# Last MLP, second layer: both halves of positions take weight rows 0 and 1, then both take rows 2 and 3

## The chip, the cores and the metric

One core of a Trainium2 chip runs the whole program. The time is the device time of one execution in microseconds (us). Fewer is better. The kernel before took 1864.22 us (median of 3 runs, 1864.22 to 1864.34).

## The reference

The program computes three blocks on 512 positions of width 1024, in float32: a convolutional mixer with a gated MLP, a retention layer with an MLP, and a chunked attention layer with an MLP, with a final RMS norm. The change touches only the last MLP, and of it only the second matrix product:

```python
def _sqrelu_mlp(h, w1, w2):
    u = jax.nn.relu(h @ w1)
    return (u * u) @ w2
...
        h = h + _sqrelu_mlp(_rmsnorm(h, mlp_norm_g[i]), mlp_w1[i], mlp_w2[i])
    return _rmsnorm(h, final_norm_g)
```

Here `w1` is 1024 x 4096 and `w2` is 4096 x 1024.

## The kernel before, in words

Every float32 product is made of three matmuls: an operand is split into a high part (`_hi`, float32r) and a low part (`_lo`, what is left), and `product` (lines 688 to 690) issues hi x hi, hi x lo and lo x hi into the same PSUM bank. ScalarE (ACT) makes the high part of a weight block (line 1198), GpSimd (POOL) subtracts it from the weights to make the low part (line 667).

The last MLP goes in 4 chunks ("turns") of 1024 hidden columns. A chunk first makes its hidden columns (8 units of 24 matmuls), then its second layer (`seven_products`), which is a 2 x 2 block product done with seven products instead of eight. Their names, in order, are b11, b21, t1, b22, t2, t3 and t4. Each has a weight block of 4 rows of 128 x 512 (k = 0 to 3), held in one of the two slots of `w_hi` and `w_lo` in turn, and 256 positions in two halves of 128. A unit is one half with all four rows, 12 matmuls, with its own PSUM bank. The units of a chunk are numbered u = 0 to 13 (b11 is 0 and 1, b21 is 2 and 3, t1 is 4 and 5, and so on).

Four PSUM banks serve these units: two (one for each half) for b11, t2, t3 and t4, two for b21, t1 and b22. So two products that follow each other, such as b21 and t1, use the same two banks. After each unit TensorE (PE) signals `unit_done`, VectorE (DVE) adds the bank into the result in SBUF (line 1941, 128x512; line 1939 where it is the first) and signals `unit_taken`; the next unit on that bank waits for it (`pe.wait_ge(unit_taken, ...)`).

DVE works in the order of `seven_rows` (line 1927 on): the add of u, and between these adds
- after u = 2 `from_psum` (line 1862, two instructions), which turns the copy of a weight block in PSUM (`in_psum`, written by ACT at line 1272) into the block of t2,
- after u = 4 and 5 `psum_lo` (line 1868), the low part of t2's rows 0 and 1, and of its rows 2 and 3, each after ACT's high part; after u = 5 `from_psum` again, for t4,
- after u = 8 and 9 `psum_lo` for t4,
- in the last chunk, from u = 10 on, `end_rows`: the sums of squares, the root and the scaling by the final norm (lines 1888, 1904, 1875 to 1883), row block by row block.

ACT converts two blocks ahead, one conversion behind each unit (`after_unit`, `convert`). A weight slot may be overwritten in rows 0 and 1 once both halves have passed them, which PE signals with `half_used`, and in rows 2 and 3 when the block is done. The blocks of raw weights are loaded by SP's queue.

All engines run their own list in order, written out by the loops of the source; nothing schedules them.

Of the kernel before, what the change touches and what calls it, by code (L numbers as in the profile page):

```python
# [24 lines left out]
P = 128  # L25
# [12 lines left out]
MLP_CHUNKS = 4  # L38
# [56 lines left out]
IN_A = ("b11", "t2", "t3", "t4")  # L95
# [69 lines left out]
def build(nc, phases, x_in, w_in, w_out, w_gate, w_up, w_down, ret_w_in, ret_w_out, att_w_in,  # L165
# [4 lines left out]
    with ctx:  # L170
# [36 lines left out]
        ps = ctx.enter_context(nc.psum_tensor("ps", [P, 8, SEQ], F32))  # L207
# [5 lines left out]
        ms, root, rc, t4 = (cols[:, 4 * k:4 * k + 4] for k in range(4))  # L213
# [48 lines left out]
        def operand(kind, k):  # L262

            if kind in ("b21", "t4"):
                cut = slice(0, 256) if kind == "b21" else slice(256, 512)
                return hh[:, k, cut], hl[:, k, cut]
            if kind in ("t1", "t2"):
                cut = slice(0, 256) if kind == "t1" else slice(256, 512)
                return hh[:, 4 + k, cut], hl[:, 4 + k, cut]
            n = ("b11", "t3", "b22").index(kind)  # L270
            return combined_hi[:, n, k, :], combined_lo[:, n, k, :]
# [22 lines left out]
        def sem(name):  # L294
            sems.append(ctx.enter_context(nc.semaphore(name)))
            return sems[-1]
# [8 lines left out]
        t_lo = sem("t_lo")  # L305
# [9 lines left out]
        w_hi = sem("w_hi")  # L315
        w_lo = sem("w_lo")
        unit_done = sem("unit_done")
        unit_taken = sem("unit_taken")
# [29 lines left out]
        half_used = sem("half_used")  # L348
# [29 lines left out]
        n_blocks = len(plan)  # L378
# [12 lines left out]
        rows_turn = plan[:rows_from].count("b11")  # L391

        def by_rows(b):

            return b >= rows_from and plan[b] in QUARTERS
# [286 lines left out]
        def _(pe):  # L682
            c = Counts(pe, sems)
            banks = [4]

            def product(o, a, b, first, last):

                nc.tensor.matmul(o, a[0], b[0], start=first, stop=False, skip_group_check=True)  # L688
                nc.tensor.matmul(o, a[0], b[1], start=False, stop=False, skip_group_check=True)  # L689
                return nc.tensor.matmul(o, a[1], b[0], start=False, stop=last, skip_group_check=True)  # L690

            def low(ahead):

                behind = lows[c.unit.n + ahead] - (c.unit.n + ahead)
                return c.unit.value(ahead + behind)

            def weights(slot, width):
                return [t[:, slot, :].rearrange("p (k c) -> p k c", c=width) for t in (wh, wl)]
# [151 lines left out]
            def quarter(kind, turn, half, banks_of):  # L850

                if kind in ("t2", "t4"):
                    pe.wait_ge(t_lo, 4 * turn + (1 if kind == "t2" else 3) + half)
                else:
                    pe.wait_ge(w_lo, low(1))
                back = {"b11": 4, "b21": 4, "t2": 8}.get(kind, 2)
                pe.wait_ge(unit_taken, c.unit.value(1 - back))
                w = weights(c.unit.n // 2 % 2, 512)
                bank = banks_of["a" if kind in IN_A else "c"][half]
                opens, ends = kind in ("b11", "b21", "t1"), kind in ("b21", "b22", "t4")  # L860
                ready = {"b11": a11_ready, "b21": a12_ready, "t4": a12_ready}.get(kind, s_ready)
                for m in range(2):
                    for k in range(4):
                        if half == 0 and m == 0:
                            pe.wait_ge(ready, 4 * turn + k + 1)
                        d = P * (half + 2 * m)
                        mm = product(ps[:, bank, 256 * m:256 * (m + 1)], [t[:, k, d:d + P] for t in w], operand(kind, k),
                                     opens and m == 0 and k == 0, ends and k == 3)
                mm.then_inc(unit_done, c.made(unit_done))
                c.unit.n += 1  # L870

            def quarter_rows(kind, turn, half, banks_of):

                def weights_ready(rows):
                    if kind in ("t2", "t4"):
                        pe.wait_ge(t_lo, 4 * turn + (1 if kind == "t2" else 3) + rows)
                    else:
                        pe.wait_ge(w_lo, low(1 + rows))

                back = {"b11": 4, "b21": 4, "t2": 8}.get(kind, 2)  # L880
                pe.wait_ge(unit_taken, c.unit.value(1 - back))
                w = weights(c.unit.n // 2 % 2, 512)
                bank = banks_of["a" if kind in IN_A else "c"][half]
                opens, ends = kind in ("b11", "b21", "t1"), kind in ("b21", "b22", "t4")
                ready = {"b11": a11_ready, "b21": a12_ready, "t4": a12_ready}.get(kind, s_ready)
                for k in range(4):
                    if half == 0:
                        if k % 2 == 0:
                            weights_ready(k // 2)
                        pe.wait_ge(ready, 4 * turn + k + 1)  # L890
                    positions = [t[:, P * half:P * (half + 1)] for t in operand(kind, k)]
                    mm = product(ps[:, bank, :], positions, [t[:, k, :] for t in w], opens and k == 0, ends and k == 3)
                    if half == 1 and k == 1:
                        mm.then_inc(half_used, c.made(half_used))
                mm.then_inc(unit_done, c.made(unit_done))
                c.unit.n += 1

            def turn_x(part, turn):

# [8 lines left out]
            def seven_products(turn):  # L908

                n = c.unit.n  # L910
                banks_of = {"a": (n % 4, (n + 1) % 4), "c": ((n + 2) % 4, (n + 3) % 4)}
                for kind in QUARTERS:
                    for half in range(2):
                        if turn >= rows_turn:
                            quarter_rows(kind, turn, half, banks_of)
                        else:
                            quarter(kind, turn, half, banks_of)
                    if turn == rows_turn + TURN_X_IN and kind in ("t3", "t4"):
                        turn_x(int(kind == "t4"), turn)
# [4 lines left out]
            for f in phases:  # L924
                if f == "mix":
# [3 lines left out]
                    for u in range(4, MIX_UNITS):  # L929
                        unit8(X)  # L930
                        for g in taps_after(u):
# [3 lines left out]
                            for m in range(2):  # L935
                                mm = nc.tensor.matmul(ps[:, 6 + m, :], tap_w[:, g % 4, m, :], upad[:, 2 + m, g:g + SEQ],
                                                      start=g == 0, stop=g == TENSOR_TAPS - 1, skip_group_check=True)
# [5 lines left out]
                    for t in range(4):  # L943
                        mm = nc.tensor.matmul(ps[:, 5, :], ones[:, :], cacc[:, t, :], start=t == 0, stop=t == 3,
                                              skip_group_check=True)
# [199 lines left out]
        def _(act):  # L1145
            c = Counts(act, sems)
# [6 lines left out]
            def convert(n=1):  # L1153

                for _ in range(n):
                    place = c.of[w_hi]
                    halves = place.n
                    if place.turn is None and halves >= 2 * n_blocks:
                        return
                    if place.turn is None and halves >= 2 * rows_from and halves % 2 == 0 and not held:  # L1160
                        b = halves // 2
                        if by_rows(b) != by_rows(b - 2):
                            held.append(b)
                            continue
                        if by_rows(b):
                            act.wait_ge(half_used, [by_rows(before) for before in range(b - 1)].count(True))
                    convert_half()
                    if held:
                        held.clear()
                        convert_half()  # L1170

            def convert_half():
# [24 lines left out]
                to = halves_of(wh[:, slot, :], half) if kind == "raw" else half_of(wh[:, slot, :], halves // 2, half)  # L1197
                nc.scalar.activation(to, source, ACT.Copy).then_inc(w_hi, c.made(w_hi))  # L1198

            def after_unit():  # L1200
                act.wait_ge(unit_done, c.next(unit_done))
                c.unit.n += 1
                convert()

            def make_root():
                act.wait_ge(to_curve, c.next(to_curve))
# [141 lines left out]
            for d in range(KT):  # L1348
                if d == 2:
                    first_rows(0, 1, first_hi)  # L1350
                if d == 4:
# [4 lines left out]
                nc.scalar.activation(xh[:, d, :], x[:, d, :], ACT.Copy, scale=prow("norm_mix_g", d)).then_inc(  # L1356
                    hi_made, c.made(hi_made))
            convert(2)
            for k in range(KT):
                if k >= 5:  # L1360
# [5 lines left out]
            for f in phases:  # L1366
                nxt = next_prep(f)
                if f == "mix":
                    make_roots()
                    for u in range(MIX_UNITS):  # L1370
# [6 lines left out]
                        if u in LONG_BEHIND:  # L1377
                            t = LONG_BEHIND[u]
                            act.wait_ge(u_ready, 1)
                            for n in range(POOL_TAPS):  # L1380
                                k = TENSOR_TAPS + n
                                nc.scalar.activation(long_piece[t - 2][n], upad[:, t, k:k + SEQ], ACT.Copy,
                                                     scale=prow("conv_b_w", 4 * k + t)).then_inc(long_scaled, 1)
                        if u in APAD_BEHIND:
                            t = APAD_BEHIND[u]
# [1180 lines left out]
```

## Time and profile before

| | |
|---|---|
| median of 3 runs | 1864.22 us |
| the profiled execution, its time | 1864.35 us |
| its span on the core | 1862.6 us |
| PE busy | 1840.3 us (99%) |
| DVE, ACT, POOL busy | 1133.1, 843.1, 944.5 us |
| granted TensorE clock | 0.999 of full |

The profile is of one execution. Times on the rows are us from the start of the span. "Idle before" is how long an engine had done nothing before the row, and what ended it. PE is busy nearly all the time, so that what decides is where PE has idle time, and what an engine that PE waits for does there. The second layers of the last MLP stand at 1564.5 to 1602.6, 1652.2 to 1690.2, 1734.2 to 1772.3 and 1816.3 to 1854.8 us.

### The profile page before, as it was taken

To read this page: it belongs to the slowest core of one execution; us is meant where nothing else is said; L and a number is where in the kernel's file an instruction comes from. 1 tells how busy PE (TensorE), PEld (TensorE's weight loads), DVE (VectorE), ACT (ScalarE), POOL (GpSimd) and SP (SyncE) were. 2 spreads that over 40 slices of the span, in tenths; PEclk is the share of its full clock that TensorE was granted. 3 is DMA by queue.
4 is the path that set the end of the run, shared out by engine and by line. 5 is a ranking of instruction groups with operands and counts; after the bars stand their busy time and mean duration, and the time that the engine had idled before them with its cause. 6 is when DMAs were issued, how large, how long until landed. Compare 5 with 4: busy or idle time off the path is not lost.

```text
span 1862.6 us, 24027 instructions
## 1 busy us (share of the span) xinstructions
PE 1840.3 (99%) x9444; PEld 1569.4 (84%) x9444; DVE 1133.1 (61%) x1816; ACT 843.1 (45%) x1318; POOL 944.5 (51%) x407
## 2 busy tenths in 40 slices
PE   9999999999999999999999999999999999999998
PEld 7778889898888888888889898998888887888886
DVE  6987775775776333433565445457777766454546
ACT  5345343342354233332454545355666645443544
POOL 5673466475443434333448566574222327674755
PEclk9999999999999999999999999999999999999999
DMA  5222414424232222222243232403333332423221
GB/s 187 91 91 68 153 51 155 151 76 151 68 113 68 91 91 91 68 91 90 83 165 114 68 136 68 136 28 99 101 101 110 103 101 80 136 78 126 91 91 57
DMA packets 142764, 187.10 MB, mean 100 GB/s; under 512 B 4000, under 2 KB 102576, under 8 KB 142528
## 3 DMA queue, kind: packets, MB, share of 16 engines
q1 hardware_dynamic: 135392, 172.76, 28.1%
q10 hardware_dynamic: 7264, 12.86, 2.4%
q8 instruction: 72, 1.18, 0.3%
q14 instruction: 36, 0.29, 0.0%
HBM read 179.28 MB, written 6.33 MB: 100 GB/s over the span
## 4 chain that ended last, share of the span: by engine, by line
PE 80%; DVE 9%; ACT 3%; issue 1%; POOL 1%; DMA 0%; ACTq 0%; DVEq 0%
PE ps L688 26%; PE ps L690 26%; PE ps L689 26%; DVE ps L2066 1%; POOL w_lo L667 1%; ACT w_hi L1198 1%; DVE work L2408 1%; DVE diagonals L1734 1%; DVE xl L1760 0%; DVE probs_t_lo L2427 0%; PE ps L1077 0%; DVE work L2421 0%; PE ps L1011 0%; DVE work L2004 0%; DVE q_hi L2398 0%
## 5 line engine op out<-in xcount | busy, mean ns | idle before, releaser
L667 POOL TENSOR_TENSOR w_lo<-raw,w_hi 128x1024 fp32r<-128x1024 f32 x244 | 591.1, 2431 | 754.9 <-ACT w_hi L1198 754.9
L688 PE MATMUL ps<-xh,w_hi 128*128 128x512 f32 x1408 | 554.0, 393 | 4.9 <-DVE xl L1760 2.7
L690 PE MATMUL ps<-xh,w_lo 128*128 128x512 f32 x1408 | 548.2, 389 | 0.0
L689 PE MATMUL ps<-xl,w_hi 128*128 128x512 f32 x1408 | 548.2, 389 | 0.0
L1198 ACT ACTIVATE w_hi<-raw 128x1024 fp32r<-128x1024 f32 x262 | 273.2, 1057 | 427.9 <-PE ps L690 397.6
L688 PEld LDWEIGHTS ps<-xh,w_hi 128*128 128x128 f32 x1408 | 264.4, 188 | 64.4 <-issue 8.0
L689 PEld LDWEIGHTS ps<-xl,w_hi 128*128 128x128 f32 x1408 | 264.4, 188 | 55.3 <-issue 1.9
L690 PEld LDWEIGHTS ps<-xh,w_lo 128*128 128x128 f32 x1408 | 264.3, 188 | 55.3
L688 PE MATMUL ps<-hid_hi,w_hi 128*128 128x256 f32 (+1 forms) x688 | 228.3, 332 | 1.8 <-DVE hid_lo L2010 0.7
L690 PE MATMUL ps<-hid_hi,w_lo 128*128 128x256 f32 (+1 forms) x688 | 227.1, 330 | 0.0
L689 PE MATMUL ps<-hid_lo,w_hi 128*128 128x256 f32 (+1 forms) x688 | 227.0, 330 | 0.0
L688 PEld LDWEIGHTS ps<-hid_hi,w_hi 128*128 128x128 f32 x688 | 130.8, 190 | 14.9 <-DVE hid_lo L2010 1.9
L690 PEld LDWEIGHTS ps<-hid_hi,w_lo 128*128 128x128 f32 x688 | 130.8, 190 | 11.9
L689 PEld LDWEIGHTS ps<-hid_lo,w_hi 128*128 128x128 f32 x688 | 130.8, 190 | 11.8 <-issue 0.2
L667 POOL TENSOR_TENSOR w_lo<-down,w_hi 128x1024 fp32r<-128x1024 f32 x40 | 96.2, 2420 | 84.2 <-ACT w_hi L1198 84.2
L1975 DVE TENSOR_TENSOR x<-x,ps 128x512 f32<-128x512 f32 x84 | 56.9, 685 | 75.5 <-PE ps L690 75.4
L667 POOL TENSOR_TENSOR w_lo<-work,w_hi 128x1024 fp32r<-128x1024 f32 x36 | 86.3, 2411 | 13.0 <-ACT w_hi L1198 13.0
L2342 DVE SCALAR_TENSOR_TENSOR work<-ps,r_bc 128x512 f32<-128x512 f32 x64 | 43.6, 690 | 79.9 <-PE ps L690 79.9
L688 PE MATMUL ps<-w_hi,xh 128*128 128x512 f32 (+1 forms) x256 | 86.6, 338 | 0.7 <-DVE work L2227 0.7
L690 PE MATMUL ps<-w_hi,xl 128*128 128x512 f32 (+1 forms) x256 | 86.0, 336 | 0.0
L689 PE MATMUL ps<-w_lo,xh 128*128 128x512 f32 (+1 forms) x256 | 86.0, 336 | 0.0
L690 PE MATMUL ps<-combined,w_lo 128*128 128x256 f32 x288 | 81.5, 283 | 0.0
(272 smaller groups left out, 3095.8 us busy)
## 6 DMA issues: line engine op xcount, KB each, us to landing
raw<-in_mlp_w_dram SPq DMA_DIRECT2D x40, 1024.0 KB, 5.4
raw<-in_ret_w_in_dram SPq DMA_DIRECT2D x24, 1024.0 KB, 5.2
work<-in_mlp_w_dram SPq DMA_DIRECT2D x16, 1024.0 KB, 5.7
raw<-in_att_w_in_dram SPq DMA_DIRECT2D x12, 1024.0 KB, 5.5
raw<-in_w_gate_dram SPq DMA_DIRECT2D x11, 1024.0 KB, 5.3
raw<-in_w_up_dram SPq DMA_DIRECT2D x11, 1024.0 KB, 5.5
raw<-in_w_in_dram SPq DMA_DIRECT2D x9, 1024.0 KB, 5.1
raw<-in_ret_w_out_dram SPq DMA_DIRECT2D x8, 1024.0 KB, 5.1
```

The costliest lines, as they stand in the source:

```text
L667: nc.gpsimd.tensor_tensor(half_of(wl[:, b % 2, :], b, half), half_of(source, b, half), half_of(wh[:, b % 2, :], b, half).bitcast(F32), ALU ...
L688: nc.tensor.matmul(o, a[0], b[0], start=first, stop=False, skip_group_check=True)
L689: nc.tensor.matmul(o, a[0], b[1], start=False, stop=False, skip_group_check=True)
L690: return nc.tensor.matmul(o, a[1], b[0], start=False, stop=last, skip_group_check=True)
L1198: nc.scalar.activation(to, source, ACT.Copy).then_inc(w_hi, c.made(w_hi))
L1734: V.reciprocal(rough, root_rows).then_inc(dve_step, c.made(dve_step))
L1975: V.tensor_tensor(tiles, tiles, ps[:, where, :].rearrange("p (m c) -> p m c", m=2), ALU.add).then_inc(unit_taken, c.made(unit_taken))
L2066: V.scalar_tensor_tensor(total if last else acc, src, w, acc, ALU.mult, ALU.add).then_inc(signal, c.made(signal))
L2342: V.scalar_tensor_tensor(hval[:, u % 2, :], bank(), 0.0, r_bc[:, :], ALU.max, ALU.mult).then_inc(unit_taken, c.made(unit_taken))
L2408: V.tensor_tensor_reduce(probs[:, h % 2, BY_QUERY[i]:BY_QUERY[i] + n], ps[:, bk, at:at + n], bias[:, h % 4, SEQ - n:SEQ], 1.0, MASKED, ALU ...
```

## The change

In the seven products of the last MLP, PE used to run half 0 with rows 0 to 3 and then half 1 with rows 0 to 3. Now it runs four quarter steps: rows 0 and 1 for half 0, rows 0 and 1 for half 1, rows 2 and 3 for half 0, rows 2 and 3 for half 1. `half_used` comes after the second quarter step instead of after the third, `unit_done` of half 0 after the third instead of after the second. The wait of half 1 for its bank stands before the second quarter step. The t4 of the last chunk keeps the old order. On ACT, the conversion of rows 0 and 1 of the blocks t1, b22, t2, t3 and t4 waits for `half_used` alone and stands before the wait for `unit_done` (`rows_passed`), where it stood behind both. No instruction is added or taken away, and DVE's, POOL's and SP's lists are as before.

```diff
-            def quarter_rows(kind, turn, half, banks_of):
+            def quarter_rows(kind, turn, banks_of):
...
-                for k in range(4):
-                    if half == 0:
-                        if k % 2 == 0:
-                            weights_ready(k // 2)
-                        pe.wait_ge(ready, 4 * turn + k + 1)
-                    positions = [t[:, P * half:P * (half + 1)] for t in operand(kind, k)]
-                    mm = product(ps[:, bank, :], positions, [t[:, k, :] for t in w], opens and k == 0, ends and k == 3)
-                    if half == 1 and k == 1:
+                steps = [(rows, half) for rows in range(2) for half in range(2)]
+                if kind == "t4" and turn == rows_turn + MLP_CHUNKS - 1:
+                    steps.sort(key=lambda step: step[1])
+                for rows, half in steps:
+                    if half == 0 and kind in ("t2", "t4"):
+                        pe.wait_ge(t_lo, 4 * turn + (1 if kind == "t2" else 3) + rows)
+                    elif half == 0:
+                        pe.wait_ge(w_lo, low(1 + rows))
+                    bank = banks_of["a" if kind in IN_A else "c"][half]
+                    if rows == 0:
+                        pe.wait_ge(unit_taken, c.unit.value(1 + half - back))
+                    for k in (2 * rows, 2 * rows + 1):
+                        if half == 0:
+                            pe.wait_ge(ready, 4 * turn + k + 1)
+                        positions = [t[:, P * half:P * (half + 1)] for t in operand(kind, k)]
+                        mm = product(ps[:, bank, :], positions, [t[:, k, :] for t in w], opens and k == 0, ends and k == 3)
+                    if rows == 1:
+                        mm.then_inc(unit_done, c.made(unit_done))
+                    elif half == 1:
                         mm.then_inc(half_used, c.made(half_used))
-                mm.then_inc(unit_done, c.made(unit_done))
-                c.unit.n += 1
+                c.unit.n += 2
...
-                        if by_rows(b):
-                            act.wait_ge(half_used, [by_rows(before) for before in range(b - 1)].count(True))
...
+            def rows_passed():
+
+                place = c.of[w_hi]
+                b = place.n // 2
+                if place.turn is not None or place.n % 2 or not 2 <= b < n_blocks or not (by_rows(b) and by_rows(b - 2)):
+                    return False
+                act.wait_ge(half_used, [by_rows(before) for before in range(b - 1)].count(True))
+                return True
+
             def after_unit():
+                ahead = rows_passed()
+                if ahead:
+                    convert()
                 act.wait_ge(unit_done, c.next(unit_done))
                 c.unit.n += 1
-                convert()
+                if not ahead:
+                    convert()
```

PE, the product t1 of the first chunk, before. `hid_hi` and `hid_lo` are the parts of the positions, `s_ready` says that they are made; a unit is 12 rows.

```order
L688 MATMUL ps<-w_hi,hid_hi 128x512 [waits s_ready,w_lo,unit_taken]
...
L688 MATMUL ps<-w_hi,hid_hi 128x512 [waits s_ready]
...
L688 MATMUL ps<-w_hi,hid_hi 128x512 [waits s_ready,w_lo]
...
L688 MATMUL ps<-w_hi,hid_hi 128x512 [waits s_ready]
...
L688 MATMUL ps<-w_hi,hid_hi 128x512 [waits unit_taken]
L689 MATMUL ps<-w_lo,hid_hi 128x512
L690 MATMUL ps<-w_hi,hid_lo 128x512
```

The same place now:

```order
L688 MATMUL ps<-w_hi,hid_hi 128x512 [waits s_ready,unit_taken,w_lo]
...
L688 MATMUL ps<-w_hi,hid_hi 128x512 [waits s_ready]
...
L688 MATMUL ps<-w_hi,hid_hi 128x512 [waits unit_taken]
...
L688 MATMUL ps<-w_hi,hid_hi 128x512
...
L688 MATMUL ps<-w_hi,hid_hi 128x512 [waits s_ready,w_lo]
L689 MATMUL ps<-w_lo,hid_hi 128x512
L690 MATMUL ps<-w_hi,hid_lo 128x512
```

The wait of half 1 for its bank stood at the 13th matmul and stands at the 7th; the wait for the low parts of rows 2 and 3 stood at the 7th and stands at the 13th.

ACT, the conversions of the same chunk from t1 on, before:

```order
L1198 ACTIVATE w_hi<-down 128x1024 [waits t1_made,half_used,unit_done]
L1198 ACTIVATE w_hi<-down 128x1024 [waits t1_made,unit_done]
L1272 ACTIVATE ps<-down 128x2048 [waits s_ready]
L1198 ACTIVATE w_hi<-raw 128x1024 [waits down_landed2,half_used,unit_done]
L1198 ACTIVATE w_hi<-raw 128x1024 [waits down_landed2,unit_done]
L1198 ACTIVATE w_hi<-ps 128x1024 [waits t2_made,half_used,unit_done]
```

And now (the copy to PSUM is line 1285 of the changed file):

```order
L1198 ACTIVATE w_hi<-down 128x1024 [waits t1_made,half_used]
L1198 ACTIVATE w_hi<-down 128x1024 [waits t1_made,unit_done]
L1285 ACTIVATE ps<-down 128x2048 [waits s_ready]
L1198 ACTIVATE w_hi<-raw 128x1024 [waits down_landed2,half_used]
L1198 ACTIVATE w_hi<-raw 128x1024 [waits down_landed2,unit_done]
L1198 ACTIVATE w_hi<-ps 128x1024 [waits t2_made,half_used]
```

The order of ACT's instructions is the same; rows 0 and 1 of a block no longer wait for `unit_done`.

## Rows read from the trace of the kernel before

**Rows 1.** Page, part 1: busy us (share of span) and instructions.
```profile
PE 1840.3 (99%) x9444; PEld 1569.4 (84%) x9444; DVE 1133.1 (61%) x1816; ACT 843.1 (45%) x1318; POOL 944.5 (51%) x407
```
**Rows 2.** Windows, first and third second layer: engines' busy us, clock, DMA.
```profile
1564.50:1602.60 38.10, 36.27 (x159) 29.27 (x159) 22.78 (x33) 20.26 (x26) 29.65 (x13) 1.00 0.33 111
...
1734.20:1772.30 38.10, 37.92 (x167) 31.09 (x166) 21.67 (x29) 18.22 (x21) 27.44 (x13) 1.00 0.34 111
```
**Rows 3.** Waits of PE, 1500 to 1863 us: total us, times, longest us.
```profile
PE ps L688 <- POOL w_lo L667: 1.2, 4, 0.7
```
**Rows 4.** Timeline of PE, t1 of the third chunk: start us, us, instruction.
```profile
1745.09 0.39 PE L688 MATMUL ps<-w_hi,hid_hi 128*128 128x512 f32 x1
...
1746.79 0.50 PE L688 MATMUL ps<-w_hi,hid_hi 128*128 128x512 f32 x1 [0.17 <-POOL w_lo L667]
...
1748.28 0.39 PE L688 MATMUL ps<-w_hi,hid_hi 128*128 128x512 f32 x1
...
1751.00 0.39 PE L688 MATMUL ps<-w_hi,combined 128*128 128x512 f32 x1
```
**Rows 5.** Timeline of DVE, third chunk, units 0 to 5.
```profile
1741.91 1.87 DVE L1941 TENSOR_TENSOR work<-work,ps 128x512 f32<-128x512 f32 x3
1744.63 2.36 DVE L1862 TENSOR_TENSOR ps<-raw,ps 128x1024 f32<-128x1024 f32 x2 [0.85 <-ACT ps L1272]
1746.90 0.68 DVE L1941 TENSOR_TENSOR work<-work,ps 128x512 f32<-128x512 f32 x1
1748.48 0.69 DVE L1941 TENSOR_TENSOR work<-work,ps 128x512 f32<-128x512 f32 x1 [0.90 <-PE ps L690]
1750.95 1.22 DVE L1868 TENSOR_TENSOR w_lo<-ps,w_hi 128x1024 fp32r<-128x1024 f32 x1 [1.78 <-ACT w_hi L1198]
1752.09 0.68 DVE L1941 TENSOR_TENSOR work<-work,ps 128x512 f32<-128x512 f32 x1
1752.69 1.22 DVE L1868 TENSOR_TENSOR w_lo<-ps,w_hi 128x1024 fp32r<-128x1024 f32 x1
```
**Rows 6.** Timeline of ACT, third chunk.
```profile
1742.72 1.88 ACT L1272 ACTIVATE ps<-down 128x2048 f32<-128x2048 f32 x1
...
1749.89 1.03 ACT L1198 ACTIVATE w_hi<-ps 128x1024 fp32r<-128x1024 f32 x1 [3.37 <-PE ps L690]
```
**Rows 7.** Timeline of PE, b21 of the first chunk.
```profile
1571.34 0.47 PE L688 MATMUL ps<-w_hi,hid_hi 128*128 128x512 f32 x1 [1.16 <-issue]
...
1573.64 0.51 PE L688 MATMUL ps<-w_hi,hid_hi 128*128 128x512 f32 x1 [0.67 <-POOL w_lo L667]
```
**Rows 8.** Timeline of DVE, first chunk, unit 3.
```profile
1579.10 0.68 DVE L1941 TENSOR_TENSOR work<-work,ps 128x512 f32<-128x512 f32 x1
```
**Rows 9.** Timelines of DVE, PEld (weight load) and PE: DVE releases PE.
```profile
1541.84 1.29 DVE L2342 SCALAR_TENSOR_TENSOR work<-ps,r_bc 128x512 f32<-128x512 f32 x2
...
1542.65 0.19 PEld L688 LDWEIGHTS ps<-xh,w_hi 128*128 128x128 f32 x1 [0.72 <-issue]
...
1542.98 0.39 PE L689 MATMUL ps<-xl,w_hi 128*128 128x512 f32 x1
```
**Rows 10.** Timeline of DVE, last chunk, adds of units 10 to 13.
```profile
1846.99 0.68 DVE L1941 TENSOR_TENSOR work<-work,ps 128x512 f32<-128x512 f32 x1
...
1849.64 0.69 DVE L1941 TENSOR_TENSOR work<-work,ps 128x512 f32<-128x512 f32 x1
...
1852.31 0.69 DVE L1941 TENSOR_TENSOR work<-work,ps 128x512 f32<-128x512 f32 x1
...
1855.36 0.69 DVE L1941 TENSOR_TENSOR work<-work,ps 128x512 f32<-128x512 f32 x1
```
**Rows 11.** Timeline of PE, last chunk: first matmul of t4.
```profile
1849.39 0.39 PE L688 MATMUL ps<-w_hi,hid_hi 128*128 128x512 f32 x1
```
**Rows 12.** Chain that ended last, its step at unit 11.
```profile
1849.64 0.70 DVE work L1941
```

More of the change, by code:

```diff
@@ L870, in quarter @@
                 c.unit.n += 1
-            def quarter_rows(kind, turn, half, banks_of):
[L874 to L878, printed above, removed]
+            def quarter_rows(kind, turn, banks_of):
                 back = {"b11": 4, "b21": 4, "t2": 8}.get(kind, 2)
-                pe.wait_ge(unit_taken, c.unit.value(1 - back))
@@ L882, in quarter_rows @@
                 w = weights(c.unit.n // 2 % 2, 512)
-                bank = banks_of["a" if kind in IN_A else "c"][half]
                 opens, ends = kind in ("b11", "b21", "t1"), kind in ("b21", "b22", "t4")
                 ready = {"b11": a11_ready, "b21": a12_ready, "t4": a12_ready}.get(kind, s_ready)
-                for k in range(4):
-                    if half == 0:
-                        if k % 2 == 0:
-                            weights_ready(k // 2)
-                        pe.wait_ge(ready, 4 * turn + k + 1)
-                    positions = [t[:, P * half:P * (half + 1)] for t in operand(kind, k)]
-                    mm = product(ps[:, bank, :], positions, [t[:, k, :] for t in w], opens and k == 0, ends and k == 3)
-                    if half == 1 and k == 1:
+                steps = [(rows, half) for rows in range(2) for half in range(2)]
@@ L912, in seven_products @@
                 for kind in QUARTERS:
[L913 to L916, printed above, removed]
+                    if turn >= rows_turn:
+                        quarter_rows(kind, turn, banks_of)
+                    else:
+                        for half in range(2):
                             quarter(kind, turn, half, banks_of)
```

## The prediction, made before the changed kernel ran

> **What bounds the kernel.** I read the page first: PE is busy 99% of the span [rows 1], so only PE's idle time, or the end behind PE, can change the total. Then the windows over the second layers of the last MLP: 37.92 of 38.10 us busy in the third, 36.27 of 38.10 in the first (rows of matmuls can be missing there, so I take PE's gaps from the timeline), clock 1.00 in both [rows 2]. The waits of PE name what these stages wait for: POOL's low parts, four times, 1.2 us in all [rows 3]. The timeline then shows each. In t1 of the third chunk the first matmul starts at 1745.09, the seventh (rows 2 and 3 of the weights) at 1746.79 after a wait for POOL; b22 starts at 1751.00 [rows 4]. From 1748.28 to 1751.00 twelve matmuls take 2.72 us, 0.2267 each, so a product of 24 takes 5.44, and t1 without a wait would have ended at 1750.53: it loses 0.47 us. The four waits of rows 3 are this one in three chunks and one more in the first. In the first chunk the wait falls in b21: its first matmul is late as well (1571.34), and the seventh, due 1.36 us later, comes at 1573.64 [rows 7]. A restart costs a little more than the row shows (t1: 1746.79 to 1748.28 is 1.49 for six matmuls, 0.13 too many), so I count the seventh as 1573.75 and the second gap as 1.0.
>
> Last, DVE, because PE's next unit on a bank waits for DVE's add. In the third chunk the adds of u = 0 to 2 stand at 1741.91; from_psum begins at 1744.63, when ACT's copy to PSUM has ended (1742.72 + 1.88) [rows 5, 6]; the add of u = 3 comes behind it at 1746.90 and ends at 1747.58. Before the change nobody is hurt: t1's half 1, which needs that bank, starts at 1748.28.
>
> **What the change removes.** The wait for rows 2 and 3 moves from the 7th to the 13th matmul of a product, 1.36 us later. POOL is late by less than that, so 0.47 us goes in each of three chunks and 1.0 in the first: 2.4 us at most. ACT's earlier conversions bring nothing: t1's two stand right behind other ACT work, up to the copy at 1742.72, and t2's first (1749.89) is used only one product later [rows 6].
>
> **What it adds, at t1.** Half 1 now wants its bank at the 7th matmul. t1 starts at 1745.09, so it wants it at 1746.45; DVE gives it at 1747.58. from_psum doesn't move earlier: its start is set by ACT's copy; the add of u = 2 moves from 1743.1 to 1743.93 (b21 starts at 1739.65; the third quarter step ends 4.08 later; DVE follows 0.20 behind, as the add of u = 4 at 1748.48 does the unit's end at 1748.28 [rows 4, 5]) and ends at 1744.62, as the copy ends. When DVE releases PE, the weight load comes 0.12 after the end of the DVE instruction (the first of two at 1541.84 ends at 1542.53, the load is at 1542.65) and the next matmul at 1542.98, so in steady terms PE restarts 0.22 behind DVE's end [rows 9]. So half 1 starts at 1747.80, three quarter steps (4.08) are left, and t1 ends at 1751.88 instead of 1751.00: **+0.88** net, the removed 0.47 counted. The second and fourth chunk have the same rows, 82 us apart: 3 x 0.88 = 2.64. In the first chunk the add of u = 3 ends at 1579.78 [rows 8], t1's half 1 at 1580.00, its end 1584.08; before it ended at 1573.75 + 4.08 + 5.44 = 1583.27: **+0.81**, with b21's gain used up in this.
>
> **What it adds, at b22 and t3.** Call E the end of t1. The add of u = 4 starts at E - 1.36 + 0.20. psum_lo follows after 0.60 and the add of u = 5 another 1.14 later (the steps 1752.09 to 1752.69 and 1750.95 to 1752.09 [rows 5]); ACT's part for psum_lo is then made. So u = 5 is added from E + 0.58 to E + 1.27, PE restarts at 1.49, and b22's half 1 wants the bank at 1.36: **+0.13**. Between t2 and t3 psum_lo stands in the same place: +0.13. Per chunk 0.26, four chunks 1.04. I bound each from below by nothing (if the load may follow closer) and from above by 0.3.
>
> All other hand-overs are near as well. Half 0 of a product is added from 4.28 to 4.97 of its 5.44 us, ready for a load 0.12 later at 5.09, and the load is wanted at 5.21; before there were 2.72 us, now 1.36. I take nothing for them. If each of the five others in a chunk failed by 0.1 that would be 2 us.
>
> [...] b21, t1 and b22 share a pair of banks; the trace before agrees that this costs nothing with 2.72 us between uses, and the sum above holds only because 1.36 us is left. [...]
>
> **What it adds, at the end.** t3 of the last chunk starts at 1843.95 (24 matmuls before 1849.39 [rows 11]), call it S. The add of u = 10 was at S + 3.04 (1846.99) and is now at S + 4.28: 1.24 later. The sums and the root that DVE makes between it and the add of u = 11 takes 2.65 (1846.99 to 1849.64), then 2.67 to u = 12 and 3.05 to u = 13 [rows 10]. Before, PE and DVE tie here: u = 11 was ready at 1849.59, u = 12 at 1852.31; u = 13, ready at 1855.03, came 0.33 late. Now DVE is late from u = 10 on, each of the three comes behind DVE's own work, and the chain that ended last already runs through DVE from u = 11 [rows 12]. So the whole **+1.24** reaches the end. t4 itself is unharmed: half 1 wants its bank at S + 8.16, u = 11 is taken at S + 7.62. Bounds: 0.9 (if 0.33 of it were slack) to 1.5.
>
> **The sum.** 2.64 + 0.81 + 1.04 + 1.24 = 5.73 us. The profiled execution took 1864.35, so 1870.1; the median of the runs shown is 0.13 lower: 1870.0. Nothing behind a chunk absorbs it, since PE has no other wait in the next chunk's first layer.
>
> **Rivals.**
> - *Not slower: the add of u = 3 isn't late.* If from_psum ran early enough for that add to end by 1746.2, t1's new wait would vanish, the removed 2.4 would count, and b22, t3 and the end cost 1.04 + 1.24: 1864.2 - 2.4 + 2.3 = 1864.1. It decides at 1.4 us earlier on DVE. For it: the waits are read from order and rows, not measured. Against it: ACT's copy ends at 1744.60 and nothing on ACT before it is released by PE's order.
> - *Half the price.* t1's stalls come, but the end and the small ones don't (DVE fits its root work into what PE leaves): 2.64 + 0.81 = 3.45, 1867.7, just within 0.2%. Against it: the chain that ended last runs through DVE there before the change too [rows 12].
> - *Every hand-over fails.* With 0.1 at the twenty others: 1872.0.
> [...]
> - *The change does nothing*: excluded by the order of PE's waits.
>
> **How the numbers follow.** Forecast (t1 and the end, with or without the small ones) 0.76; every hand-over 0.07; half the price 0.07; not slower 0.08; clock 0.02. A measurement of this kernel tells 0.2%, 3.7 us, from no change. Slower by more than that: 0.76 + 0.07 + 0.02, less a little for a forecast case that falls short, 0.82; within 0.2%: 0.16; faster, which would need all of these stages' idle time, 0.02. The range goes from just under the half price, 1867.0, to every hand-over with the end's upper bound, 1872.6.
>
> **What would show it.** In the changed profile: the 0.17 us waits of PE for POOL gone, and in each chunk a wait of PE's L688 for DVE's add (the L1941 in before's lines) of about 1.1 to 1.4 us at the 7th matmul of t1; b22 starting near 1752 minus the shift of earlier chunks; short waits at the 7th matmul of b22 and t3; from chunk to chunk 82.1 us before (1734.2 to 1816.3), about 83.2 now; the add of u = 10 in the last chunk 4.3 to 4.4 us behind t3's first matmul, and from there to the end the same distance as before. The prediction is wrong if PE shows no wait for that add, or if the last add follows PE's last matmul as closely as before (0.5 us).

## The result, and the profile after

The changed kernel takes 1869.43 us (median of 8 runs, 1869.27 to 1871.87) against 1864.28 us before (8 runs). The ratio is 1.0028, 95% interval 1.0018 to 1.0039: slower by 5.15 us. The profiled execution took 1869.27 us, its span 1867.5 us. I had predicted 1870.0 us.

The page hardly shows it. PE was busy 1840.3 us and is busy 1840.8 us; the loss is idle time, and part of it lies behind PE. First the waits of PE from 1500 us on (in all us, times, longest), the view of [rows 3]:

```profile
PE ps L688 <- DVE work L1954: 4.5, 4, 1.5
PE ps L688 <- POOL w_lo L667: 1.2, 1, 1.2
```

L1954 is DVE's add, L1941 before. The four waits of 1.2 us in all for POOL are gone. The one of 1.2 us that stands here is the late first matmul of b21 in the first chunk. It is as it was; the profile of the kernel before only puts it down to "issue", a wait for nothing that the profile shows:

```profile
PE ps L688 <- issue: 1.2, 1, 1.2
```

New are the four waits for an add. The timeline of PE in the third chunk shows where (start, duration, instruction, in brackets the idle time and its end), as [rows 4] did before:

```profile
1749.34 0.50 PE L688 MATMUL ps<-w_hi,hid_hi 128*128 128x512 f32 x1 [1.02 <-DVE work L1954]
...
1753.55 0.39 PE L688 MATMUL ps<-w_hi,combined 128*128 128x512 f32 x1
1754.91 0.46 PE L688 MATMUL ps<-w_hi,combined 128*128 128x512 f32 x1
1755.21 0.39 PE L689 MATMUL ps<-w_lo,combined 128*128 128x512 f32 x1
...
1759.09 0.39 PE L688 MATMUL ps<-w_hi,hid_hi 128*128 128x512 f32 x1
```

The seventh matmul of t1 starts 1.41 us behind the sixth; 0.23 is the step without a wait, and it was 0.56 in the kernel before, where this matmul waited for POOL. b22, from 1753.55 to 1759.09, lasts 5.54 instead of 5.44: its seventh matmul is followed by the eighth after 0.30. DVE in the same chunk, which answers to [rows 5]:

```profile
1743.61 1.28 DVE L1954 TENSOR_TENSOR work<-work,ps 128x512 f32<-128x512 f32 x2
1745.63 0.69 DVE L1954 TENSOR_TENSOR work<-work,ps 128x512 f32<-128x512 f32 x1 [0.75 <-PE ps L690]
1746.33 2.36 DVE L1875 TENSOR_TENSOR ps<-raw,ps 128x1024 f32<-128x1024 f32 x2
1748.60 0.68 DVE L1954 TENSOR_TENSOR work<-work,ps 128x512 f32<-128x512 f32 x1
1752.39 0.69 DVE L1954 TENSOR_TENSOR work<-work,ps 128x512 f32<-128x512 f32 x1 [3.11 <-PE ps L690]
1753.00 1.22 DVE L1881 TENSOR_TENSOR w_lo<-ps,w_hi 128x1024 fp32r<-128x1024 f32 x1
1754.13 0.68 DVE L1954 TENSOR_TENSOR work<-work,ps 128x512 f32<-128x512 f32 x1
```

The add of u = 3 (1748.60) still stands behind from_psum and ends at 1749.28; PE's matmul follows at 1749.34. from_psum itself (1746.33) begins when both the add of u = 2 (1746.32) and ACT's copy to PSUM (1746.30) have ended. The add of u = 5 (1754.13) stands behind psum_lo and ends at 1754.81, 0.10 before b22's seventh matmul is due.

The windows over the first and third second layer (busy us of PE, PEld, DVE, ACT, POOL, clock, DMA; they answer to [rows 2]) show the clock still full:

```profile
1564.20:1605.70 41.50, 38.88 (x170) 31.23 (x169) 23.54 (x33) 20.22 (x26) 32.08 (x14) 1.00 0.29 102
1735.90:1775.50 39.60, 38.58 (x170) 31.31 (x169) 21.85 (x29) 18.33 (x21) 27.86 (x13) 1.00 0.32 107
```

The end, on DVE in the last chunk ([rows 10] before):

```profile
1852.03 0.69 DVE L1954 TENSOR_TENSOR work<-work,ps 128x512 f32<-128x512 f32 x1 [1.44 <-PE ps L690]
...
1854.64 0.69 DVE L1954 TENSOR_TENSOR work<-work,ps 128x512 f32<-128x512 f32 x1
...
1857.23 0.68 DVE L1954 TENSOR_TENSOR work<-work,ps 128x512 f32<-128x512 f32 x1
...
1860.27 0.69 DVE L1954 TENSOR_TENSOR work<-work,ps 128x512 f32<-128x512 f32 x1
```

From the add of u = 10 to the add of u = 13 it is 8.24 us (8.37 before, where PE was the later one at some of them), but the first of them, at 1852.03, is 4.38 us behind t3's first matmul (1847.65), where it was 3.04.

### The profile page after: what moved, and what is told of

Same layout as the page of the kernel before. It is cut to its first block, busy times and chain, and to the rows that moved or that the text cites. A ratio compares the mean times of both kernels' runs of the same rounds, so it can differ in the third digit from the quotient of the medians.

```text
span 1867.5 us, 24028 instructions
## 1 busy us (share of the span) xinstructions
PE 1840.8 (99%) x9444; PEld 1568.6 (84%) x9444; DVE 1133.5 (61%) x1816; ACT 843.3 (45%) x1318; POOL 944.2 (51%) x407
## 4 chain that ended last, share of the span: by engine, by line
PE 82%; DVE 8%; ACT 2%; issue 1%; POOL 1%; ACTq 0%; DVEq 0%
PE ps L688 27%; PE ps L690 26%; PE ps L689 26%; DVE ps L2079 1%; DVE diagonals L1747 1%; DVE xl L1773 0%; ACT work L1627 0%; PE ps L1079 0%; DVE probs_t_lo L2440 0%; PE ps L1013 0%; DVE work L2421 0%; DVE work L2434 0%; DVE work L2017 0%; ACT w_hi L1198 0%; POOL w_lo L667 0%
```

## Experiments

All ran in the kernel's whole program, with the kernel before on the same chip beside them. Its medians there were 1864.26 (first four), 1864.49 (next four) and 1864.67 us (last four). All ratios below are to these. Because these medians differ by 0.4 us, a difference from the changed kernel is taken from how far each lies from the kernel before beside it (the changed kernel: +5.15 us).

**1. PE's part alone.** The four quarter steps on PE; `after_unit` and `convert` of ACT as before.

```diff
+                        if by_rows(b):
+                            act.wait_ge(half_used, [by_rows(before) for before in range(b - 1)].count(True))
...
-            def rows_passed():
...
             def after_unit():
-                ahead = rows_passed()
-                if ahead:
-                    convert()
                 act.wait_ge(unit_done, c.next(unit_done))
                 c.unit.n += 1
-                if not ahead:
-                    convert()
+                convert()
```

> PE's four quarter steps as in the changed kernel; ACT's conversions wait and stand as before the change. Theory (PE's order makes PE wait for DVE's adds, and DVE's end sequence starts later; ACT's part is worth nothing): as the changed kernel, 1869.4 us, within 0.5. Rival (ACT's earlier conversions collide with DVE or POOL and cause the loss): 1863 to 1865.

Measured: 1873.25 us, ratio 1.0047 (1.0033 to 1.0060), 3.8 us slower than the whole change. This is neither what the theory nor what the rival gave. The wait at t1 is as it was, but b22 and t3 now lose much more. DVE and PE in the third chunk:

```profile
1754.26 0.69 DVE L1943 TENSOR_TENSOR work<-work,ps 128x512 f32<-128x512 f32 x1 [3.12 <-PE ps L690]
1755.32 1.22 DVE L1870 TENSOR_TENSOR w_lo<-ps,w_hi 128x1024 fp32r<-128x1024 f32 x1 [0.37 <-ACT w_hi L1200]
1756.46 0.68 DVE L1943 TENSOR_TENSOR work<-work,ps 128x512 f32<-128x512 f32 x1
```
```profile
1757.19 0.50 PE L688 MATMUL ps<-w_hi,combined 128*128 128x512 f32 x1 [0.25 <-DVE work L1943]
```

ACT converts t2's rows only after `unit_done` of u = 4, which now comes a quarter step later; psum_lo waits 0.37 us for it, and the add of u = 5 is behind psum_lo. b22 lasts 6.00 us instead of 5.54. t3 loses the same. 0.46 us at eight places is 3.7 of the 3.8 us.

**2. ACT's part alone.** PE's old order, ACT as changed.

> PE's order as before the change, ACT's conversions of rows 0 and 1 follow half_used alone as in the changed kernel. Theory: as before, 1864.3 us, within 0.5, with the same four waits of PE for POOL. Rival (ACT's part costs): up to 1869.

Measured: 1864.53 us, ratio 1.0001 (0.9992 to 1.0010), and PE's waits for POOL are the four of before. Alone, ACT's part does nothing. With PE's part it is worth 3.8 us: the two edits don't add up.

**3. The add of unit 3 first.** The changed kernel, one line of DVE's order:

```diff
-                    if u == 2:
+                    if u == 3:
                         dve.wait_ge(t1_copied, c.next(t1_copied))
                         dve.wait_ge(down_landed[2], 16 * (turn + 1))
                         from_psum(down(turn)[2])
```

> The changed kernel, but DVE adds unit 3 before the first from_psum instead of behind it; nothing else is moved. Theory (t1's half 1 waits for this add because from_psum, 2.27 us, stands before it): the wait of PE at t1 goes, 3 x 1.29 + 1.6 = 5.5 us off: 1863.9 us; t2_made comes 0.7 later, which nobody waits for. Rival (the bank is late for another reason, or t1 then waits for POOL's low parts, or each hand-over at 1.36 us costs by itself): less than 2 us off, above 1867.4.

Measured: 1863.96 us, ratio 0.9999 (0.9990 to 1.0008): 5.5 us less than the changed kernel, as the theory said. The waits of PE from 1500 us on:

```profile
PE ps L688 <- POOL w_lo L667: 1.2, 1, 1.2
PE ps L688 <- DVE work L2355: 0.3, 1, 0.3
```

The waits for the add of u = 3 are gone and none has come in their place; the small losses at b22 and t3 stay (the one of 0.3 us lies ahead of these stages, before the change too).

**4. t3 of the last chunk in the old order.**

```diff
-                if kind == "t4" and turn == rows_turn + MLP_CHUNKS - 1:
+                if kind in ("t3", "t4") and turn == rows_turn + MLP_CHUNKS - 1:
```

> The changed kernel, but in the last chunk t3 too keeps the old order (half 0 with all rows, then half 1), as t4 does. Theory (DVE's end sequence starts with the add of unit 10 and reaches the end in full): the add of unit 10 comes 1.3 us earlier relative to t3's start, the end 1.2 us earlier: 1868.2 us. Rival (the end is set by PE's last matmul, the distance is slack): no change, 1869.4.

Measured: 1868.30 us, ratio 1.0021 (1.0012 to 1.0031): 1.1 us less than the changed kernel. DVE adds u = 10 at 1850.59, 2.92 us behind t3's first matmul (1847.67) instead of 4.38, so 1.46 us earlier. Of this 0.25 is lost again up to the add of u = 13 (at 1859.08, 8.49 us behind instead of 8.24), mostly where DVE now waits for PE at u = 11; the other 1.2 us reach the end:

```profile
1850.59 0.69 DVE L1954 TENSOR_TENSOR work<-work,ps 128x512 f32<-128x512 f32 x1
...
1853.36 0.69 DVE L1954 TENSOR_TENSOR work<-work,ps 128x512 f32<-128x512 f32 x1 [0.20 <-PE ps L690]
```

**5. DVE's list fitted to the new order.** 3 and 4 together, and both `psum_lo` behind the odd unit:

```diff
-                    if u in (4, 5):
-                        psum_lo(block + 4, half)
+                    if u == 5:
+                        psum_lo(block + 4, 0)
+                        psum_lo(block + 4, 1)
...
-                    if u in (8, 9):
-                        psum_lo(block + 6, half)
+                    if u == 9:
+                        psum_lo(block + 6, 0)
+                        psum_lo(block + 6, 1)
```

> The changed kernel with DVE's list fitted to it: unit 3 is added before the first from_psum, both psum_lo of a block stand behind the add of the odd unit (5 and 9), and t3 of the last chunk keeps the old order. Theory (the loss is DVE's other work in front of the adds that PE waits for, and the late start of the end sequence): 1863.96 of the run with unit 3 first, less 1.13 for the end, less 8 x 0.095 for the small waits: 1862.1 us, faster than before. Rival (the gains overlap, or the later low parts make PE wait at t2 and t4): 1863 to 1865.

Measured: 1862.13 us, ratio 0.9988 (0.9979 to 0.9997). It beats both kernels: 7.5 us less than the change, 2.4 less than before. The adds now follow PE, each in its quarter step (DVE, third chunk):

```profile
1742.30 0.69 DVE L1954 TENSOR_TENSOR work<-work,ps 128x512 f32<-128x512 f32 x1 [0.75 <-PE ps L690]
1743.66 0.69 DVE L1954 TENSOR_TENSOR work<-work,ps 128x512 f32<-128x512 f32 x1 [0.67 <-PE ps L690]
1744.27 2.35 DVE L1875 TENSOR_TENSOR ps<-raw,ps 128x1024 f32<-128x1024 f32 x2
```

**6. Only the `psum_lo` moved**, the rest as changed.

> The changed kernel, but both psum_lo of a block stand behind the add of the odd unit (5 and 9), not one behind each unit. Theory: the small waits of PE at b22 and t3 go, 8 x 0.095: 1868.7 us; the 1.3 us waits at t1 stay. Rival (the small extra is the cost of the new hand-over itself, not of psum_lo): no change, 1869.4.

Measured: 1868.83 us, ratio 1.0024 (1.0015 to 1.0033), 0.8 less than the changed kernel; b22 and t3 last 5.44 us again, and the waits at t1 are there. The difference of the medians is small against the spread of the runs (1868.33 to 1871.04); the trace carries this point.

**7 and 8. One more instruction in front of the add of unit 3**, in the changed kernel and in the kernel before:

```diff
+                    if u == 3:
+                        V.tensor_copy(qh[:, 0, :], r_bc[:, :])
                     dve.wait_ge(unit_done, c.next(unit_done))
```

> The changed kernel with one more DVE instruction of 128 x 512 (about 0.65 us; it copies a tile to one that nobody reads) in front of the add of unit 3 in each chunk. Theory (this add is what PE waits for at t1): each chunk 0.65 longer, 2.6 in all: 1872.0 us. Rival (the wait at t1 is for something else that ends at the same time): below 1870.5.

> The kernel before with the same additional DVE instruction in front of the add of unit 3. Theory: before, that add has 0.35 us to spare (0.4 in the first chunk), so 0.3 in three chunks and 0.25 in the first are left: 1865.4 us. Rival (the old order has a whole unit to spare): 1864.3.

Measured: 1885.39 us, ratio 1.0109 (1.0094 to 1.0124), and 1871.77 us, ratio 1.0038 (1.0024 to 1.0052). Both far more than expected, because the instruction took 2.41 us (2.45 in the kernel before), not 0.65. So the size was wrong, and the trace shows why it costs even more in the changed kernel. DVE, POOL and PE of the changed kernel with it, first chunk:

```profile
1578.94 2.40 DVE L1950 CAST q_hi<-r_bc 128x512 fp32r<-128x512 f32 x1
```
```profile
1578.73 4.84 POOL L667 TENSOR_TENSOR w_lo<-raw,w_hi 128x1024 fp32r<-128x1024 f32 x2
```
```profile
1581.99 0.80 PE L688 MATMUL ps<-w_hi,hid_hi 128*128 128x512 f32 x1 [3.75 <-DVE work L1956]
1582.59 0.63 PE L689 MATMUL ps<-w_lo,hid_hi 128*128 128x512 f32 x1
1583.01 0.63 PE L690 MATMUL ps<-w_hi,hid_lo 128*128 128x512 f32 x1
```

PE stood idle for 3.75 us, and then its matmuls start 0.43 us apart instead of 0.23, until 1587.28. The granted clock from 1579 to 1588 us is 0.62 of full. In the kernel before the same instruction made PE wait 1.5 us in each chunk, and no matmul was slow: the granted clock is 1.00 in the 8 us from just ahead of each wait.

**9 and 10. The same with an instruction of the add's own form**, which takes the time of an add:

```diff
                     dve.wait_ge(unit_taken, c.unit.value(-1))
+                    if u == 3:
+                        V.tensor_tensor(qh[:, 0, :], r_bc[:, :], ps[:, where, :], ALU.add)
```

> The changed kernel with one more DVE instruction in front of the add of unit 3 in each chunk, of the add's own form (128 x 512, one operand in PSUM; its result is read by nobody), 0.61 us from start to start. Theory (this add is what PE waits for at t1): 4 x 0.61 longer: 1871.9 us, and TensorE's clock stays full. Rival (the wait is for something else that ends at the same time): below 1870.5.

> The kernel before with the same additional instruction in front of the add of unit 3. Theory: this add has 0.35 us to spare in three chunks and 0.4 in the first, so 0.26 and 0.2 are left: 1.0 in all: 1865.3 us. Rival (a whole unit to spare): 1864.3.

Measured: 1873.91 us, ratio 1.0049 (1.0035 to 1.0063), 4.1 us more than the changed kernel; and 1865.24 us, ratio 1.0003 (0.9994 to 1.0012). The wait of PE at t1 grew by 0.58 to 0.60 in each chunk, 1.02 to 1.62 in the third:

```profile
1753.30 0.50 PE L688 MATMUL ps<-w_hi,hid_hi 128*128 128x512 f32 x1 [1.62 <-DVE work L1956]
```

That is the predicted 2.4 us, so it is this add that PE waits for. Nearly all of the rest, 1.6 us in the trace, is again the clock, in the first chunk alone, where PE had been idle for 1.14 us and now is for 2.04 more. The granted clock is 0.50 of full from 1582 to 1585 us, and from 1581.51 to 1585.15 nine steps from matmul to matmul take 3.64 us instead of 2.04:

```profile
1580.71 0.50 PE L688 MATMUL ps<-w_hi,hid_hi 128*128 128x512 f32 x1 [2.04 <-DVE work L1956]
1581.05 0.40 PE L689 MATMUL ps<-w_lo,hid_hi 128*128 128x512 f32 x1
...
1581.83 0.63 PE L689 MATMUL ps<-w_lo,hid_hi 128*128 128x512 f32 x1
1582.26 0.63 PE L690 MATMUL ps<-w_hi,hid_lo 128*128 128x512 f32 x1
```

So my expectation that the clock would stay full was wrong there. In the old order PE loses only 0.06 to 0.09 us in each chunk, 0.3 of the 0.6 us between the medians, a difference that is within the interval: the add had more room than the 0.35 us I gave it. I had counted from the moment when the weight load was due, but here a load that came just ahead of its matmul was early enough. In the profile of this run the add ended at 1748.63, the load began at 1748.68 instead of 1748.51, and the matmul due at 1748.74 started then.

**11. The fitted kernel without ACT's part.**

> As the kernel with DVE's list fitted (unit 3 first, both psum_lo behind the odd unit, t3 of the last chunk in the old order), but ACT's conversions wait for unit_done as before the change. Theory (in the run with PE's part alone ACT's late conversions cost 3.8 us only because psum_lo, which waits for them, stood in front of an add that PE waits for): 1862.1 us as with ACT's part, within 0.5. Rival (PE waits for the converted rows themselves): 1864 or more.

Measured: 1862.73 us, ratio 0.9990 (0.9981 to 0.9999), against 0.9988 with ACT's part. The difference in the ratios is well inside the intervals, and the traces show the same waits of PE. So ACT's late conversions hurt in experiment 1 only through psum_lo in front of an add.

**12. The kernel before with the add of unit 3 first.**

> The kernel before, with unit 3 added before the first from_psum. Theory (nobody waited for this add in the old order): 1864.3 us, within 0.3, PE's four waits for POOL as before. Rival (the gain of the fitted kernels comes from DVE's order alone, not from it together with PE's): 1862 to 1863.

Measured: 1864.88 us, ratio 1.0000 (0.9991 to 1.0009), PE's waits as before. The reordering on DVE is worth 5.5 us in the new order and nothing in the old.

## Why the prediction was right, step by step

- *The removed waits*: right. The three at t1 are gone, and b21 of the first chunk has no second one. They were worth 2.4 us, and experiment 5 gets 2.4 us in all: its second layer is 1.01 us shorter than before in the first chunk and 0.47 in the third, the two sizes of the prediction.
- *t1*: right in mechanism and size. b21 and t1 together lasted 11.35 us and now 12.20 in the third chunk, +0.85 against +0.88; in the first chunk from b21's first matmul to b22's it was 11.96 and is 12.77, +0.81 as predicted. Experiment 3 takes the cause away and gets the sum back, 9 makes it larger in step.
- *b22 and t3*: right in place, too large in size. 0.10 instead of 0.13 at each, 0.75 us instead of 1.04. Experiment 6 removes them. The term rested on a restart 0.22 behind DVE's end, which was read after a long wait. Where the add ends 0.1 ahead of the due matmul, as here, only about 0.1 is lost.
- *The other hand-overs cost nothing*: right. t4 follows t3 on the same two banks with 1.36 us between uses and nothing else on DVE in between; in the third chunk it lasts from 1770.05 to 1775.49, 5.44 us as before. In experiment 5 no product of these stages waits for an add. So two products in turn on one pair of banks cost nothing by themselves here.
- *The end*: right in mechanism, a little too large in size. The add of u = 10 comes 4.38 instead of 3.04 behind t3's first matmul, 1.34 later. 0.09 of it is t3's own wait, counted above. From there to the add of u = 13 it is 0.13 less than before, which the prediction took as unchanged. That leaves 1.12 against 1.24. Experiment 4 gives 1.1 back.
- *ACT's part brings nothing*: right for the old order (experiment 2) and with DVE's list fitted (experiment 11), wrong for the change itself. Within the change it prevents a loss of 3.8 us, which the prediction had in its sum without seeing it: it said in half a sentence that ACT's part for psum_lo is then made.
- *The sum*: the stages of the last MLP give 4.0 us until t3 of the last chunk (from 1843.95 to 1847.65, counted with the 0.3 us by which PE was earlier ahead of these stages, at 1564.22 instead of 1564.54, where both kernels do the same) and 1.2 at the end, 5.2, against 5.7 predicted and 5.15 measured between medians. Of the 0.5 between 5.7 and 5.2, 0.3 is the shorter small waits, 0.1 the t1 term and 0.1 the end. What lies between 5.2 and 5.15 is not resolved.
- *The signs*: PE's waits at t1 are 1.02 us in three chunks and 1.46 in the first, on both sides of the 1.1 to 1.4 that I gave for all. From the third chunk to the fourth it is 83.1 us (1735.91 to 1819.01), 83.2 expected. The last add comes 1.6 us behind the end of PE's last matmul, 0.5 before.
- *A fall of the clock, given 0.02*: there was none, at gaps of 1.0 to 1.5 us; granted is 1.00 of full in the windows over the first and third second layer. Experiments 7 and 9 show that it was near: with 0.6 us more idle time in the first chunk (2.04 instead of 1.46) the granted clock is 0.50 from 1582 to 1585 us. Whether the idle time of b21 just ahead counts there wasn't tried.

## What to carry over

When a producer is given finer steps, look at what the consumer's list has between the two acknowledgements: here the time between uses of a bank went from 2.72 to 1.36 us, and a 2.27 us instruction pair that had been hidden stood between two adds. The list of the consumer has to be turned with the producer's. The add of u = 3 first gained nothing alone (experiment 12), the new order of PE with DVE's list as it was lost 5 us, the two together broke even (experiment 3), and with psum_lo and the last t3 fitted too they gained 2.4 (experiment 5). And an edit that does nothing alone can be what keeps another one cheap: undo parts from the whole, not only add them to the start.

## What I had not expected of the hardware

- A copy of 128 x 512 float32 from SBUF to SBUF on DVE (a CAST to float32r in the trace) took 2.40 to 2.46 us, all eight times in experiments 7 and 8, while an add of the same size with one operand in PSUM took 0.68 in the same place. Each time POOL had begun an instruction 0.2 us earlier, and the copy ended 0.3 us behind the end of it (1578.94 + 2.40 against 1578.73 + 2.33). Why its end follows that of the POOL instruction is not shown, and the copy without POOL beside it wasn't run.
- TensorE went to a lower clock (granted 0.50 of full, 0.43 instead of 0.23 us from matmul to matmul) after idle times of 3.75 and 3.35 us, and after 2.04 us that followed another 1.14 us by some 7 us. The granted clock is 0.50 of full from 1582 to 1587 us in experiment 7 and from 1582 to 1585 in experiment 9. It stayed full (1.00) after 1.62 us in experiment 9, 1.55 in experiment 8 and 1.46 in the changed kernel. In the first chunk of experiment 7 the slow steps lasted about 5 us, in that of experiment 9 about 3. In the third chunk of experiment 7 the slow steps began only 1.3 us behind the restart, after the same 3.3 us idle as in the second and fourth, where they began at once.
